# A recurrence on TensorE: operands in the other partition half, and a chunk chain of state matrices

## The reference

```python
def step(S, inp):
    r_t, w_t, k_t, v_t, kk_t, a_t = inp
    sa = jnp.einsum('bhvk,bhk->bhv', S, -kk_t)
    S = S * w_t[:, :, None, :] + sa[..., None] * (kk_t * a_t)[:, :, None, :] + v_t[..., None] * k_t[:, :, None, :]
    return S, jnp.einsum('bhvk,bhk->bhv', S, r_t)
```

## Time and profile before

| | us |
|---|---|
| median of three runs (lowest, highest) | 3049.85 (3047.79, 3052.39) |
| the profiled execution | 3052.54 |
| its span, first to last instruction | 3050.5 |
| PE busy in the span | 2834.7 |
| DVE busy | 1373.1 |
| POOL busy | 942.2 |
| ACT busy | 679.0 |
| granted TensorE clock, mean | 0.976 of 2.4 GHz |

### The profile page before, as it was taken

One profiled execution on the slowest core, in us unless ns is written; L12 is line 12 of the kernel. 1 busy time (PEld: TensorE's weight loads), 2 busy tenths in 40 slices (PEclk: granted clock), 3 DMA queues, 4 the chain that ended last, 5 costly groups with the idle time before them and its releaser, 6 DMA issues. The chain is left out here.

```text
span 3050.5 us, 47144 instructions
## 1 busy us (share of the span) xinstructions
PE 2834.7 (93%) x19588; PEld 2242.0 (73%) x19588; DVE 1373.1 (45%) x1372; ACT 679.0 (22%) x958; POOL 942.2 (31%) x417
## 2 busy tenths in 40 slices
PE   7999999999999999999988899999998899898887
PEld 6777788878888888888776677766676676666775
DVE  7755422234422132124657433353363463444588
ACT  3433320011210000001323344421121121112231
POOL 4222224443444444344433111031121111213365
PEclk9999999999999999999999999999999999998998
DMA  3000001121111111111221000010101011002343
GB/s 125 28 28 28 28 28 48 48 97 48 48 48 48 48 48 48 48 48 55 64 83 61 28 14 14 35 50 23 39 30 39 34 33 43 33 26 92 104 151 103
DMA packets 40746, 156.06 MB, mean 51 GB/s; under 512 B 4640, under 2 KB 5152, under 8 KB 39200
## 3 DMA queue, kind: packets, MB, share of 16 engines
q1 hardware_dynamic: 31392, 110.21, 11.2%
q10 hardware_dynamic: 9216, 43.78, 3.8%
HBM read 133.00 MB, written 20.97 MB: 50 GB/s over the span
## 5 line engine op out<-in xcount | busy, mean ns | idle before, releaser
L2309 POOL TENSOR_TENSOR w_hi<-w_raw,one 128x1024 fp32r<-128x1024 f32 x199 | 388.9, 1954 | 2055.0 <-PE dps L283 1508.2
L283 PE MATMUL dps<-h_hi,w_hi 128*128 128x512 f32 x1904 | 609.4, 396 | 46.5 <-issue 11.1
L283 PE MATMUL dps<-h_lo,w_hi 128*128 128x512 f32 x1904 | 602.6, 392 | 0.0
L283 PE MATMUL dps<-h_hi,w_lo 128*128 128x512 f32 x1904 | 600.8, 391 | 0.0
L2311 POOL TENSOR_TENSOR w_lo<-w_raw,w_hi 128x1024 fp32r<-128x1024 f32 x199 | 525.7, 2641 | 15.6
L283 PEld LDWEIGHTS dps<-h_hi,w_hi 128*128 128x128 f32 x1904 | 359.1, 190 | 135.4 <-issue 40.4
L283 PEld LDWEIGHTS dps<-h_lo,w_hi 128*128 128x128 f32 x1904 | 361.3, 190 | 76.2 <-issue 0.5
L283 PEld LDWEIGHTS dps<-h_hi,w_lo 128*128 128x128 f32 x1904 | 360.8, 189 | 76.1
L300 PE MATMUL dps<-h_lo,w_hi 128*128 128x512 f32 x352 | 131.1, 441 | 18.4 <-DVE rw_akt L1871 7.3
L300 PE MATMUL dps<-h_hi,w_lo 128*128 128x512 f32 x352 | 124.4, 423 | 19.5 <-DVE rw_akt L1883 9.5
L300 PE MATMUL dps<-h_hi,w_hi 128*128 128x512 f32 x352 | 127.1, 432 | 10.7 <-DVE rw_akt L1883 6.2
(11 more groups left out here) (349 smaller groups left out, 4172.9 us busy)
## 6 DMA issues: line engine op xcount, KB each, us to landing
w_raw<-w_stream SPq DMA_DIRECT2D x200, 512.0 KB, 3.7
x_again<-x_t ACTq DMA_DIRECT2D x2, 4096.0 KB, 14.1
gates<-gate_out ACTq DMA_DIRECT2D x16, 512.0 KB, 2.7
tmp<-gates ACTq DMA_DIRECT2D x16, 512.0 KB, 4.5
x_t<-x_res ACTq DMA_DIRECT2D x4, 1024.0 KB, 4.3
out_t<-x_again SPq DMA_DIRECT2D x16, 256.0 KB, 2.0
back<-branches ACTq DMA_DIRECT2D x7, 512.0 KB, 9.5
x_res<-x_t ACTq DMA_DIRECT2D x2, 1536.0 KB, 12.4
```

The costliest lines, as they stand in the source:

```text
L283: mm = k.nc.tensor.matmul(k.dps[0:rows, pair, h * HALF:(h + 1) * HALF], w[:, slot, sub + t, 0:rows], x(t)[:, h * HALF:(h + 1) * HALF], sta ...
L2309: g.tensor_tensor(k.w_hi[:, s], k.w_raw[:, s], ones, ALU.mult).then_inc(k.sem("w_hi_done"), 1)
```

## The change

Some matrices are written into the partition half of the other head: a product's output goes to the columns of the other head (OTHER) or stays (SAME), and its operands are read from where they lie. `each` and `mul` take that as an argument. The mask product is made twice, as lt (SAME) and lt_x (OTHER). xt, t1, kkp_tm and akv lie in the other half. Where two products use different quarters, their matmuls are issued in turn, chunk by chunk, into two banks: lt and lt_x, l and kkp_tm, ke_tm and akv, x and xt of levels 1 to 4, u0 and the first part of n, w1 and the first part of y.

The chunk loop is rewritten. With w1 and u0 (copied with scale -1) PE makes, for all chunks at once, n = ke.v + be.u0, m = w1.be and r = w1.arbt. VectorE (rw_turn_dve) builds turn = diagonal of the chunk's decay + m, and adds r to rp. A chunk is then one product turn.s and one VectorE addition of n. The y products of chunk c - 1 stand behind the chain product of chunk c. ScalarE copies one bank more (n), and akv after be_tm and ke_tm. FILL_T and FILL_X become 5 and 5; there are 5 dense matmuls before n, 6 before the loop's first wait, 2 between chunks.

```diff
-    for name, room in (("w1_t", "lt"), ("u0", "xm"), ("u", "t1"), ("s", "akt"), ("y", "akv")):
+    for name, room in (("w1", "lt"), ("u0", "xm"), ("turn", "t1"), ("s", "akt"), ("n", "kkp_tm"), ("y", "akv")):
...
-PRODUCTS = Steps("rw_product", ["rk", "lt", "l", "ak_t", "rb_t", "rk_t", "kkp_tm", "v_tm", "akv", "be_tm", "ke_tm"] + LEVEL_NAMES
-                 + ["u0", "w1_t"] + [f"{n}{c}" for c in range(NC) for n in ("w1s", "ds")])
+PRODUCTS = Steps("rw_product", ["rk", "lt", "lt_x", "l", "kkp_tm", "ak_t", "rb_t", "rk_t", "v_tm", "be_tm", "ke_tm", "akv"]
+                 + LEVEL_NAMES + ["u0", "w1", "n", "m", "r"] + [f"ms{c}" for c in range(NC)])
 VALUES = Steps("rw_value", ["rkv", "lt", "xt_part", "xt0", "x_part", "x0", "ak_t", "rb_t", "rk_t"] + LEVEL_NAMES
-               + ["s_in"] + [f"{n}{c}" for c in range(NC) for n in ("u", "s")])
-COPIES = Steps("rw_copy", ["kkp_tm", "v_tm", "akv", "be_tm", "ke_tm", "u0", "w1_t"])
+               + ["decay", "m", "r", "s_in"] + [f"s{c}" for c in range(NC)])
+COPIES = Steps("rw_copy", ["kkp_tm", "v_tm", "be_tm", "ke_tm", "akv", "u0", "w1", "n"])
...
-FILL_MASKS, FILL_T, FILL_X, FILL_START, FILL_U, FILL_S, FILL_Y = 2, 4, 6, 4, 3, 5, 8
+FILL_MASKS, FILL_T, FILL_X, FILL_N, FILL_M, FILL_S = 2, 5, 5, 5, 6, 2
...
+    def mul(out, at, c, lhs, rhs, start=True, stop=True):
+        (lhs, ins), rhs = lhs, rhs[0]
+        for h in range(2):
+            mm = k.nc.tensor.matmul(out[at[h], c * CH:(c + 1) * CH], lhs[ins[h], c, :], rhs[ins[h], c, :],
+                                    start=start, stop=stop, skip_group_check=True)
+        return mm
+    def turn(out, at, c, lhs):
+        for head, to in zip(HEADS, at):
+            mm = k.nc.tensor.matmul(out[to, c * CH:(c + 1) * CH], lhs(head, c), const(k, "pair_ident")[head],
+                                    start=True, stop=True, skip_group_check=True)
+        return mm
...
-    each_chunk("lt", made["bq"], made["kkp"])
-    each_chunk("l", made["kkp"], made["bq"])
+    for c in range(NC):
+        a = mul(bank(k, "lt"), SAME, c, channel("bq"), channel("kkp"))
+        b = mul(bank(k, "lt_x"), OTHER, c, channel("bq"), channel("kkp"))
+    a.then_inc(product, 1)
+    b.then_inc(product, 1)
     if before is not None:
         rw_result_pe(k, pe, before, "mean")
     fill(FILL_MASKS - 1)
-    free("ak_t")
-    free("rb_t")
-    fill(1)
-    each_chunk("ak_t", made["kq"], made["kkp"])
-    each_chunk("rb_t", made["bq"], made["rp"])
-    fill(FILL_MASKS - 1)
-    free("rk_t")
+    free("l")
     free("kkp_tm")
     fill(1)
-    each_chunk("rk_t", made["kq"], made["rp"])
-    turned("kkp_tm", made["kkp"])
+    for c in range(NC):
+        a = mul(bank(k, "l"), SAME, c, channel("kkp"), channel("bq"))
+        b = turn(bank(k, "kkp_tm"), OTHER, c, chunk("kkp"))
+    a.then_inc(product, 1)
+    b.then_inc(product, 1)
     fill(FILL_MASKS - 1)
-    free("v_tm")
+    free("ak_t")
     fill(1)
-    for c in range(NC):
-        t = slice(u.g * HALF + c * CH, u.g * HALF + (c + 1) * CH)
-        mm = both(k, bank(k, "v_tm")[:, c * CH:(c + 1) * CH], k.rw_v[:, t], const(k, "pair_ident"))
-    mm.then_inc(product, 1)
+    each("ak_t", SAME, channel("kq"), channel("kkp"))
+    fill(FILL_MASKS - 1)
+    free("rb_t")
+    free("rk_t")
+    fill(1)
+    each("rb_t", SAME, channel("bq"), channel("rp"))
+    each("rk_t", SAME, channel("kq"), channel("rp"))
...
+    free("ke_tm")
+    free("akv")
+    fill(1)
+    for c in range(NC):
+        a = turn(bank(k, "ke_tm"), SAME, c, chunk("ke"))
+        b = mul(bank(k, "akv"), OTHER, c, same("akt"), same("v_tm"))
+    a.then_inc(product, 1)
+    b.then_inc(product, 1)
     for l in LEVEL_STEPS:
         fill(FILL_T - 1)
         free(f"t{l}")
         u.wait(pe, VALUES, "x0" if l == 1 else f"x{l - 1}")
         fill(1)
-        each_chunk(f"t{l}", m["lt"], m["xm"])
+        each(f"t{l}", OTHER, same("lt"), same("xm"))
         fill(FILL_X - 1)
         u.wait(pe, VALUES, f"t{l}")
         if l < LEVELS:
             free(f"x{l}")
         free(f"xt{l}")
         fill(1)
-        if l < LEVELS:
-            each_chunk(f"x{l}", m["xt"], m["t1"])
-        each_chunk(f"xt{l}", m["t1"], m["xt"])
+        if l == LEVELS:
+            each(f"xt{l}", OTHER, other("t1"), other("xt"))
+        else:
+            for c in range(NC):
+                a = mul(bank(k, f"x{l}"), SAME, c, other("xt"), other("t1"))
+                b = mul(bank(k, f"xt{l}"), OTHER, c, other("t1"), other("xt"))
+            a.then_inc(product, 1)
+            b.then_inc(product, 1)
+    y = k.aps[:, 3, :]
     fill(FILL_T - 1)
     free("u0")
-    free("w1_t")
+    free("w1")
     u.wait(pe, VALUES, f"xt{LEVELS}")
     u.wait(pe, COPIES, "akv")
-    fill(1)
-    each_chunk("u0", m["xt"], m["akv"])
-    each_chunk("w1_t", m["kkp_tm"], m["xt"])
-    assert filled >= 6 * KT
-    fill(FILL_START)
-    u.wait(pe, COPIES, "w1_t")
-    for c in range(NC):
-        at = slice(c % 2 * HD, (c % 2 + 1) * HD)
-        u.wait(pe, VALUES, f"s{c - 1}" if c else "s_in")
-        fill(FILL_S)
-        both(k, k.aps[:, 0, at], m["w1_t"][:, c, :], m["s"][:, c, :]).then_inc(product, 1)
-        both(k, k.aps[:, 1, at], m["ke_tm"][:, c, :], m["v_tm"][:, c, :], stop=False)
-        u.wait(pe, VALUES, f"u{c}")
-        fill(FILL_U)
-        both(k, k.aps[:, 1, at], m["be_tm"][:, c, :], m["u"][:, c, :], start=False).then_inc(product, 1)
     if before is not None:
         before.wait(pe, Y_COPIES, "std")
-    fill(FILL_Y)
+    fill(1)
     for c in range(NC):
-        t = slice(c * CH, (c + 1) * CH)
-        both(k, k.aps[:, 3, t], m["s"][:, c, :], made["rp"][:, c, :], stop=False)
-        both(k, k.aps[:, 3, t], m["v_tm"][:, c, :], m["arkt"][:, c, :], start=False, stop=False)
-        mm = both(k, k.aps[:, 3, t], m["u"][:, c, :], m["arbt"][:, c, :], start=False)
-    mm.then_inc(k.sem("rw_y_product"), 1)
+        a = mul(bank(k, "u0"), SAME, c, other("xt"), other("akv"))
+        mul(bank(k, "n"), HEADS, c, same("ke_tm"), same("v_tm"), start=c == 0, stop=False)
+    a.then_inc(product, 1)
+    for c in range(NC):
+        a = mul(bank(k, "w1"), SAME, c, other("xt"), other("kkp_tm"))
+        mul(y, HEADS, c, same("v_tm"), same("arkt"), start=c == 0, stop=False)
+    a.then_inc(product, 1)
+    fill(FILL_N - 1)
+    u.wait(pe, COPIES, "w1")
+    fill(1)
+    for c in range(NC):
+        mm = mul(bank(k, "n"), HEADS, c, same("be_tm"), same("u0"), start=False)
+    mm.then_inc(product, 1)
+    each("m", HEADS, same("w1"), same("be_tm"))
+    each("r", HEADS, same("w1"), same("arbt"))
+    fill(max(FILL_M, 6 * KT + 1 - filled) - 1)
+    u.wait(pe, VALUES, "m")
+    fill(1)
+    def result(c):
+        mul(y, HEADS, c, same("u0"), same("arbt"), start=False, stop=False)
+        return mul(y, HEADS, c, (m["s"], HEADS), channel("rp"), start=False)
+    for c in range(NC):
+        if c:
+            fill(FILL_S - 1)
+        u.wait(pe, VALUES, f"s{c - 1}" if c else "s_in")
+        if c == 1:
+            u.wait(pe, VALUES, "r")
+        fill(1)
+        both(k, bank(k, "m")[:, c % 2 * HD:(c % 2 + 1) * HD], m["turn"][:, c, :], m["s"][:, c, :]).then_inc(product, 1)
+        if c:
+            result(c - 1)
+    result(NC - 1).then_inc(k.sem("rw_y_product"), 1)
     fill(6 * KT * len(tiles))
...
+    rw_turn_dve(k, dve, first)
...
+    rw_turn_dve(k, dve, last)
...
+def rw_turn_dve(k, dve, u):
+    v = k.nc.vector
+    made = k.sem("rw_value")
+    turn, rp = k.half["turn"], k.ahead["rp"][u.g]
+    pc = k.rw_pc[:, u.g * NC:(u.g + 1) * NC].rearrange("p (c t) -> p c t", t=1).to_broadcast([P, NC, HD])
+    v.tensor_tensor(turn[:, :, :], masked(k, "pair_ident"), pc, ALU.mult).then_inc(made, 1)
+    u.wait(dve, VALUES, "decay")
+    u.wait(dve, PRODUCTS, "m")
+    v.tensor_tensor(turn[:, :, :], turn[:, :, :], chunks(bank(k, "m")), ALU.add).then_inc(made, 1)
+    u.wait(dve, PRODUCTS, "r")
+    v.tensor_tensor(rp[:, :, :], rp[:, :, :], chunks(bank(k, "r")), ALU.add).then_inc(made, 1)
 def rw_chunks_dve(k, dve, u):
     v = k.nc.vector
     made = k.sem("rw_value")
     m = k.half
     v.tensor_copy(m["s"][:, 0, :], k.rw_s[:, :]).then_inc(made, 1)
-    u.wait(dve, VALUES, "s_in")
-    u.wait(dve, COPIES, "u0")
+    u.wait(dve, COPIES, "n")
     for c in range(NC):
-        at = slice(c % 2 * HD, (c % 2 + 1) * HD)
-        u.wait(dve, PRODUCTS, f"w1s{c}")
-        v.scalar_tensor_tensor(m["u"][:, c, :], k.aps[:, 0, at], -1.0, m["u0"][:, c, :], ALU.mult, ALU.subtract).then_inc(made, 1)
-        u.wait(dve, PRODUCTS, f"ds{c}")
-        if c:
-            u.wait(dve, VALUES, f"s{c - 1}")
-        pc = k.rw_pc[:, u.g * NC + c:u.g * NC + c + 1]
+        u.wait(dve, PRODUCTS, f"ms{c}")
         out = m["s"][:, c + 1, :] if c < NC - 1 else k.rw_s[:, :]
-        v.scalar_tensor_tensor(out, m["s"][:, c, :], pc, k.aps[:, 1, at], ALU.mult, ALU.add).then_inc(made, 1)
+        v.tensor_tensor(out, m["n"][:, c, :], bank(k, "m")[:, c % 2 * HD:(c % 2 + 1) * HD], ALU.add).then_inc(made, 1)
```

(55 more changed lines are left out.)

2 lines of the change are left out of this document (removed).

## The result

| | before | after |
|---|---|---|
| median of the runs, us | 3050.3 (3047.8 to 3052.4) | 2938.6 (2935.3 to 2939.4) |
| ratio | | 0.963, 95% interval 0.962 to 0.965 |
| profiled execution, us (span) | 3052.5 (3050.5) | 2935.3 (2933.5) |
| eight halves, us | 674.0 | 557.5 |

The kernel is 112 us faster. The forecast was 2939 us. Its steps were not all that good: two terms were 7 us too long together, and smaller ones were 2 us too short. In this table before has one run more than in the table ahead of the prediction. "After" is the changed kernel. The first line is the page of after (as the earlier trace rows), the others are its windows of halves (as the earlier trace rows).

The account below looks back on a forecast made before the run. It took TensorE (PE), busy 93% of the span, as the bound. Halves of 3 x 70.4 + 3 x 74.3 + 69.7 + 59 = 562.8 us against 674.0 gave 2941 profiled, 2939 median; range 2925 to 2963.

Parts of the forecast that it names:

- Price of a pair of blocks: Two interleaved 64x64 products for all chunks on different quarters of PE: 0.93 us together, as long as one alone.
- Rival A: Quarters sharing rows take turns: each of 72 interleaved pairs costs 0.93 us more, 67 us, so 3006; chance 0.20.
- Rival B: Quarters overlap partly, starts limited somewhere between 29 and 14.5 ns: 34 us more, 2973; chance 0.18.
- My estimate of 48 us more: Interleaved pairs under the skill's 25 ns issue floor: 64 starts, 1.6 us a pair, 48 us over 72 pairs, giving 2987.
- Rival C: Changing quarter inside a block drains the array, 16 times a pair, 1152 in all: slower, 3213; chance 0.05.
- Up to the first level: Start of a half to its first t product: 16.7 us instead of 17.56; 0.8 shorter in the very first half.
- Levels, second halves: Levels in a pair's second half, decided by PE: 4.84 us each against 5.81 before; x1 to xt5 20.3.
- Levels, first halves: Levels in a pair's first half, decided by VectorE: each gains only 0.33 us; x1 to xt5 24.2 instead of 25.49.
- From u0 to the chain: From u0 to the first chain product: 8.1 us, with no PE wait for VectorE's preparation or the state copy.
- Chain: Chunk loop of one product and one VectorE addition: period 1.16 us without stall; eight chunks and last results 8.8 us.
- Tail and last half: After the chunk loop 51 dense matmuls at full pace, 11.7 us; the last half, waiting on VectorE at lower clock, 59.
- The sum: All eight halves: 562.8 us against 674.0, 111 less; profiled execution 2941, median 2939.

Follow-up runs that it names:

- e2_same_quarters: The changed kernel, still interleaved, with each pair's second product put on the same two quarters as its first (output wrong): 2994.2 us, ratio 0.982 against before.
- e3_old_loop: The changed kernel's quarters and interleaving up to xt5, with u0, w1, chunk loop and y of the kernel before: 3011.7 us, ratio 0.988 against before.

## Why the prediction was right, step by step

- **Price of a pair of blocks.** Predicted 0.93 us, measured 0.94. Rival A (0.93 more a pair) is what e2_same_quarters looks like, 55 us slower than after. Rival B, a limit of starts between 29 and 14.5 ns, falls with the same rows: 64 records start in 0.94 us, 14.7 ns each. In the estimate by the Trainium skill (TensorE: Matmul & The Clock Gate, "Back-to-back issue gap") I had applied its 25 ns to every record. For records the trace shows less: 14.7 ns on the mean, and four records start within 0.02 us (the rows at 2235.32 and 2235.33). A matmul has two of them here, and 29 ns per matmul on the mean doesn't contradict it; which records belong to one matmul the rows don't tell, so how far apart single matmuls start stays open. My estimate of 48 us more would have needed the floor to hold for records, and it doesn't.
- **Rival C**, a drain at each change of quarter, would have shown in the pair: 0.94 leaves nothing for 16 changes.
- **Up to the first level.** Predicted 16.7 us, measured 16.17 in seven halves (15.13 in the very first, for 15.9). This term was mis-sized by 0.5 to 0.8 a half, 4.5 in all. The trace of before has a dense matmul at 2254.67 and the next at 2255.48 with 0.31 of idle time, waiting for VectorE's mask before rk_t: 0.81 for what takes 0.227. I had carried that stall over. The new order has three more dense matmuls there and no such wait.
- **Levels, second halves.** 4.84 us predicted, 4.89 measured (x at 18.63, 23.53, 28.42, 33.31 us).
- **Levels, first halves.** Predicted x1 to xt5 24.2, measured 23.27. VectorE's turn-round was right: from one subtraction of xt to the next three levels gain 0.37, 0.34 and 0.33 us, and the way from the first x to the first such subtraction 0.33; these are the four steps of 0.33 of the forecast. Left out was 0.85 in the last level: there the product that makes rw_out took 2.06 us in before and 1.22 in after. A split of GpSimd ran there in both, in before until 2290.06 and in after until 2255.14, and the product ended 0.55 behind it each time. It had begun 1.5 us before the split's end in before and 0.7 in after. So this part of the gain is luck of place.
- **From u0 to the chain.** 8.1 predicted, 8.14 to 8.16 measured in PE-bound halves, and no wait for m or the state: VectorE had copied s at xt5 + 9.6 (2268.06), and PE asked at xt5 + 10.6. The forecast had 9.8 and 10.3; by its own terms the second is 2.42 + 8.1 = 10.5. The one wait for the state (1.5 us) is in the last half, which has no dense matmuls.
- **Chain.** Period 1.16, whole stretch 8.83 for 8.8. The split of the gain is a little off: 79 us was given to chain and y, and 32 to the blocks and the stall at the loop's start. e3_old_loop puts 38 on blocks and prologue and 73 on the rest, the stall included.
- **Tail and last half.** 51 matmuls in 11.7 us; the last half took 58.8 for 59, at a mean clock of 0.85, the same as before.
- **The sum.** 562.8 predicted, 557.5 measured. The prologue was 4.5 too long and the first halves' levels 2.8 (three halves by about 0.93); the levels' 0.05, the switches and the rest give back 2. The profiled execution was therefore 6 us below my 2941, and the median only by chance nearer to 2939: after's profiled run was its fastest. That the forecast meets the median to the microsecond is luck; what was right is the mechanism and its unit prices.
